# A first stage with its loads in another order and a ring of three, and a joining stage with modulation columns made by one transpose

## The chip, the cores and the metric

The kernel runs on one core of a Trainium2 chip. The metric is the device time of one execution in microseconds (us), lower is better. Its engines are TensorE (PE in the rows, PEld its weight loads), VectorE (DVE), ScalarE (ACT), GpSimd (POOL) and SyncE (SP). SP only issues transfers, ACT and POOL issue some of theirs.

## What the kernel computes

Two layers of a hybrid backbone over 512 latent tokens (rows of `x`) and 256 context tokens (`ctx`), each row 1024 wide, all in float32. Each layer has two sub-layers, and ahead of each of them the rows are normalised and modulated by values computed from a conditioning vector:

```
def rmsnorm(x, g):
    y = xf * lax.rsqrt(jnp.mean(xf * xf, axis=-1, keepdims=True) + EPS)
    return (y * g.astype(jnp.float32)).astype(x.dtype)

def modulate(h, shift, scale):
    return h * (1.0 + scale) + shift
...
def ab_mixer(...):
    pc = jnp.split((hc @ w_in).astype(jnp.float32), AB_SPLITS, axis=-1)
    pl = jnp.split((hl @ w_in).astype(jnp.float32), AB_SPLITS, axis=-1)
...
def mla_project(h, w_in, q_g, kv_g, w_uq, w_ukv, cs):
    p = h @ w_in
...
def hier_moe(...):
    return (jax.nn.silu(xb @ w_gate[e]) * (xb @ w_up[e])) @ w_down[e]
```

The modulation values (`mods`: per layer six vectors of 1024, once for the latent stream and once for the context stream) are the product of silu(c) with `ada_w`, which has 1024 x 6144 entries per layer, plus `ada_b`. Layer 0 is the retention and RG-LRU mixer followed by a mixture of 32 experts with two per token. Layer 1 is latent attention (MLA) followed by a second mixture. The output of a mixture goes back into the stream as `x = x + gate * (w0*y0 + w1*y1)`, where `y0` and `y1` are the rows of the token's two experts.

## The kernel before

Stages follow one another, each in a `Scope` that ends with a barrier of all engines: `ab_project` (the first stage), retention, output projection, routing and experts of layer 0, `combine` of layer 0 (here the joining stage), MLA, routing and experts of layer 1, `combine` of layer 1. A tile is 128 tokens: tiles 0 and 1 are context, 2 to 5 latent. `c.X` holds the six tiles of the stream, `hT` the normalised rows transposed (model dimension on partitions).

**First stage, `ab_project`.** It computes three things. (1) The modulation columns of the first sub-layer: `ada_step(kk, buf)` multiplies silu(c) with one chunk of `ada_w` (1 MB), eight chunks (round 0, `ada_first`) to 2048 columns. The result gets its bias (L713), is transposed (L568) and becomes `scale` and `shift` (L717, L719). (2) The rows: ACT squares each of the six tiles (L629) and takes the root after three tiles and after six (L631), DVE makes the inverse root and scales the tile into `xn` (L703), PE transposes it (L555, `x_transposes`), ACT and DVE copy it out into `hT` (L635, L706). `after` says behind which ada chunk PE has the transposes of which tile. Then L642 (ACT) and L727 (DVE) multiply `hT` by `scale` and add `shift`. (3) The projection in 40 groups, in the fixed order of `groups`: first 16 channel groups (L587; blocks 4 and 5 of `ab_w_in`, context with 256 and latent with 512 columns in turn), then 24 row groups (L583). `BEFORE` says behind which row groups PE has the gate matmuls (L602) of the RG-LRU units, whose scans run on DVE.

The other 40 chunks of `ada_w` (rounds 1 to 5) go through a ring of buffers in `c.X`, whose rows are no longer needed once they are scaled (SP waits for `scaled`). `ADA_AT[n]` is the index of the group behind which PE takes chunk n. SP walks through the groups in the same order: when chunk n is used, it issues chunk n + RING into the freed buffer, and `clear_slots(n)`, 384 KB of zeros written to `ys`.

SP's queue at the start is: eight ada chunks, the small loads of `tables.sync` (two of them `lru_lambda`, turned to columns by the transfer itself, element by element), weight blocks 0 and 1 (2 MB each, L437), nine more small loads of that kind (`cw`, `gb`), `cs`, the wait for `scaled`, ring chunks 0 and 1, the gate weights. ACT's queue has `c`, `c_ctx`, the six tiles of rows (3 MB, `load_rows`), biases and `gcol`.

**Joining stage, `combine` of layer 0.** Per tile: POOL gathers two rows per token from `ys` (L2228, three buffers), ACT weighs the first (L2244), DVE adds the second (L2269), multiplies by the gate (L2271), adds to `c.X` (L2272). `NormModulate` then normalises: ACT L158 and L161, DVE L94 to L99 and L267 (multiplies with the inverse root and with (1 + scale) * g, laid out in rows of 1024 on all partitions, `mb`, prepared by L255), POOL L276 adds the shift, PE transposes (L289), ACT copies out both halves (L298, L305). DVE has for tile t the three operations of the join, then `scale` of tile t-1. The next stage begins when the last copy is done and the barrier is passed.

## Time and profile before

| | us |
|---|---|
| median of 3 executions | 2185.58 |
| lowest and highest | 2184.8, 2187.6 |
| the profiled execution, its own time | 2187.3 |
| its span in the profile | 2185.6 |

In the span PE is busy for 1713.1 us (78%), DVE for 705.5 us, ACT for 435.5 us, POOL for 259.8 us, and the 16 DMA engines move 260 GB/s on average. The mean granted clock of TensorE is 0.899 of full speed. Shares are averages over stages of different kinds. The rows below cut out two stages: the first one up to 381 us, and the joining one from 1118 to 1187 us.

### The profile page before, as it was taken

How to read it: one execution, taken by the hardware profiler on the slowest of the kernel's cores; microseconds unless marked ns; L12 is line 12 of the kernel's file. 1: busy time of each engine (PE TensorE's matmuls, PEld its weight loads, DVE VectorE, ACT ScalarE, POOL GpSimd, SP SyncE). 2: the span in 40 equal slices, each digit the busy share in tenths (PEclk: the TensorE clock that was granted, in tenths of full speed). 3: DMA queues.
4: the chain of work that ended last, by engine and by line, in shares of the span. 5: the costliest groups of instructions: out<-in, count | busy, mean ns of one | idle time of the engine just before them, and what ended most of it. 6: DMA issues, size and time to landing. Idle time of an engine off the chain costs nothing. (4 is left out here: it accounts for less than half of the span.)

```text
span 2185.6 us, 25873 instructions
## 1 busy us (share of the span) xinstructions
PE 1713.1 (78%) x9070; PEld 895.1 (41%) x9071; DVE 705.5 (32%) x1254; ACT 435.5 (20%) x802; POOL 259.8 (12%) x350
## 2 busy tenths in 40 slices
PE   5999999799499789998614899999938789855651
PEld 2443344645244334444303545555434334433330
DVE  2403675633311111112136227776331111111114
ACT  3102323311001110111113114554101101111112
POOL 1002350301100000001013110000111000000001
PEclk8999999899599999999865899999958999987885
DMA  9767653500799999999963002000169999999993
GB/s 320 239 246 250 217 175 120 199 26 39 315 385 361 413 418 412 424 398 403 419 269 123 2 0 87 1 1 8 54 254 389 414 410 406 413 413 410 414 413 137
DMA packets 105452, 568.10 MB, mean 260 GB/s; under 512 B 22728, under 2 KB 40904, under 8 KB 65568
## 3 DMA queue, kind: packets, MB, share of 16 engines
q1 hardware_dynamic: 90544, 521.94, 60.5%
q0 software_dynamic: 7744, 26.22, 3.4%
q10 hardware_dynamic: 7088, 18.92, 2.2%
q8 instruction: 48, 0.79, 0.1%
q14 instruction: 28, 0.23, 0.0%
HBM read 525.55 MB, written 41.50 MB: 259 GB/s over the span
## 5 line engine op out<-in xcount | busy, mean ns | idle before, releaser
L1927 PE MATMUL exp_gps<-moew_wg,all_hT 128*64 128x512 f32 (+1 forms) x480 | 238.6, 621 | 35.4 <-DMA moew_wu<-in_moe_w_up 33.1
L1921 PE MATMUL exp_gps<-moew_wg,all_hT 128*32 128x256 f32 x1088 | 160.5, 460 | 104.3 <-DMA moew_wu<-in_moe_w_up 97.9
L1928 PE MATMUL exp_ups<-moew_wu,all_hT 128*64 128x512 f32 (+1 forms) x480 | 237.3, 618 | 0.0
L583 PE MATMUL abp_ps<-ab_w,all_hT 128*128 128x512 f32 x384 | 169.6, 597 | 0.6 <-PE abp_ps L587 0.3
L1921 PE MATMUL exp_ups<-moew_wu,all_hT 128*32 128x256 f32 x1088 | 160.2, 460 | 0.0
L1921 PEld LDWEIGHTS exp_gps<-moew_wg,all_hT 128*32 128x32 f32 x1088 | 79.1, 131 | 182.5 <-issue 139.0
L1927 PEld LDWEIGHTS exp_gps<-moew_wg,all_hT 128*64 128x64 f32 (+1 forms) x480 | 77.7, 166 | 169.7 <-issue 169.7
L1955 PE MATMUL exp_yps<-moew_wd,all_hT 128*64 128x512 f32 (+1 forms) x240 | 117.3, 606 | 20.4 <-issue 20.4
L2047 DVE TENSOR_TENSOR all_hT<-all_hT,exp_ups 64x512 f32<-64x512 f32 (+1 forms) x30 | 20.7, 690 | 343.6 <-ACT all_hT L1997 343.6
L1957 PE MATMUL exp_yps<-moew_wd,all_hT 128*64 128x512 f32 (+1 forms) x240 | 116.8, 603 | 0.0
L583 PEld LDWEIGHTS abp_ps<-ab_w,all_hT 128*128 128x128 f32 x384 | 71.6, 190 | 98.5 <-issue 98.3
L1421 PE MATMUL att_sc<-mla_KT,mlak_QT 96*128 96x384 f32 x256 | 100.5, 517 | 2.0 <-PEq L75 2.0
L1928 PEld LDWEIGHTS exp_ups<-moew_wu,all_hT 128*64 128x64 f32 (+1 forms) x480 | 78.5, 166 | 50.9 <-issue 50.9
L1884 POOL COPY exp_idx<-all_tok 128x1 int32 (+1 forms) x64 | 11.7, 182 | 734.9 <-DVEq L2034 734.2
L2045 DVE TENSOR_TENSOR all_hT<-all_hT,exp_ups 64x256 f32<-64x256 f32 x34 | 14.4, 425 | 253.7 <-ACT all_hT L1995 253.7
L1905 PE MATMUL exp_xps<-all_ident,all_hT 128*128 128x128 f32 x512 | 74.5, 290 | 24.8 <-DMA all_hT<-h_rows,exp_idx 24.8
L587 PE MATMUL abp_ps<-all_hT,ab_w 128*128 128x256 f32 (+1 forms) x256 | 89.4, 506 | 1.3 <-DVE all_hT L727 1.0
L1905 PEld LDWEIGHTS exp_xps<-all_ident,all_hT 128*128 128x128 f32 x512 | 64.3, 194 | 58.3 <-issue 33.2
L1949 PE MATMUL exp_yps<-moew_wd,all_hT 128*32 128x256 f32 x1088 | 69.0, 395 | 14.8 <-issue 12.1
L1493 DVE TENSOR_REDUCE att_nmax<-att_sc 128x1 f32<-128x768 f32 x64 | 61.3, 957 | 50.2 <-PE att_sc L1421 50.2
L1997 ACT ACTIVATE all_hT<-exp_gps 64x512 f32<-64x512 f32 (+1 forms) x30 | 17.8, 593 | 298.3 <-PE exp_ups L1928 298.3
L2064 DVE COPY exp_y<-exp_yps 64x512 f32<-64x512 f32 (+1 forms) x30 | 20.8, 693 | 163.2 <-PE exp_yps L1957 163.2
(399 smaller groups left out, 2572.0 us busy)
## 6 DMA issues: line engine op xcount, KB each, us to landing
moew_wg<-in_moe_w_gate SPq DMA_DIRECT2D x64, 2048.0 KB, 24.7
moew_wu<-in_moe_w_up SPq DMA_DIRECT2D x64, 2048.0 KB, 30.0
moew_wd<-in_moe_w_down SPq DMA_DIRECT2D x64, 2048.0 KB, 31.3
all_X<-in_ada_w SPq DMA_DIRECT2D x40, 1024.0 KB, 6.2
ab_w<-in_ab_w_in SPq DMA_DIRECT2D x6, 2048.0 KB, 9.1
ys<-abp_zero SPq DMA_DIRECT2D x32, 384.0 KB, 7.1
ys<-exp_y ACTq DMA_DIRECT2D x13, 512.0 KB, 8.7
ab_rows<-in_ada_w SPq DMA_DIRECT2D x6, 1024.0 KB, 12.0
```

What stands on the lines that cost most here:

```text
L583: last = nc.tensor.matmul(ps[i % RB][:], hT[:, kk, what * P:(what + 1) * P], w[n % S][:, kk, :], start=(kk == 0), stop=(kk == KD - 1))
L587: last = nc.tensor.matmul(ps[i % RB][:, 0:m], w[n % S][:, kk, ct * P:(ct + 1) * P], hT[:, kk, o:o + m], start=(kk == 0), stop=(kk == KD - 1))
L1421: last = nc.tensor.matmul(sc[n % 2][:, b, 0:HALF], k.QT[0:QD, h, t * P:(t + 1) * P], k.KT[0:QD, h, b * HALF:(b + 1) * HALF], start=True, s ...
L1493: V.tensor_reduce(nmax[:, n % R:n % R + 1], sc[n % 2][:, :, 0:HALF], mybir.AxisListType.XY, ALU.max, negate=True).then_inc(mx, 1)
L1905: last = nc.tensor.transpose(xps[k // 4][:, k % 4, :], x_by[q][:, k, :], c.ident[:])
L1921: last = nc.tensor.matmul(bank[lo + j * Q:lo + (j + 1) * Q, 0:HC], x[:, k, 0:Q], wt[:, k, j * HC:(j + 1) * HC], start=(k == 0), stop=(k == ...
L1927: nc.tensor.matmul(gps[0:rows, :], x[:, k, 0:rows], w.g[q][:, k, :], start=(k == 0), stop=(k == KD - 1))
L1928: last = nc.tensor.matmul(ups[at:at + rows, :], x[:, k, 0:rows], w.u[q][:, k, :], start=(k == 0), stop=(k == KD - 1))
L1949: last = nc.tensor.matmul(yps[j // 2][j * Q:(j + 1) * Q, 0:HC], hT[:, k, 0:Q], w.d[q][:, k, j * HC:(j + 1) * HC], start=(k == 0), stop=(k ...
L1955: nc.tensor.matmul(yps[0][0:rows, :], hT[:, k, 0:rows], w.d[q][:, k, 0:512], start=(k == 0), stop=(k == HT_N - 1))
L1957: last = nc.tensor.matmul(yps[1][at:at + rows, :], hT[:, k, 0:rows], w.d[q][:, k, 512:1024], start=(k == 0), stop=(k == HT_N - 1))
L2064: nc.vector.tensor_copy(y[q][0:rows, 512:1024], yps[1][at:at + rows, :]).then_inc(y_dve, 1)
```

## The change

The text calls it new attention together with the first stage in another order and a new joining stage. The diff has nothing in the attention itself.

- `ab_project`: the rows are loaded first on SP's queue, ahead of the ada chunks, and no longer on ACT's. Weight block 0 comes directly behind the ada chunks. The ring has three buffers, and `ADA_AT` places the eight chunks of a round behind five groups as 1, 2, 2, 2, 1 and no longer 2, 2, 2, 1, 1. The transposes of the rows stand earlier among the ada steps (`after`).
- The small parameters (`gcol`, `cw`, `gb`, `lru_lambda`) are loaded as contiguous rows into one tile `laid` (56 x 128) by five transfers of ACT's queue, transposed by one PE instruction and copied once by DVE into `pcols`. PE has the wait for these loads at the head of its queue, ahead of all ada steps, and DVE waits for the transpose ahead of its first inverse.
- `combine_into_mla` takes the place of `combine` for layer 0. ACT multiplies the tile by its inverse root, PE transposes it, ACT copies both halves out, and scale and shift are applied to `hT` afterwards by columns, odd columns on ACT and even ones on DVE, context after the context tiles, latent at the end. The columns come from one transpose of `laid` (40 x 128). POOL only gathers, and `mb` and its preparation are gone.

```diff
-        cw = s.sb("cw", [P, CONV + 1, LT])
-        gb = s.sb("gb", [P, 4, LT])
+        NG = KD
+        NW = NG + CONV * LT
+        NC = NW + LT
+        NB = NC + 4 * LT
+        NL = NB + 2 * LT
+        laid = s.sb("laid", [NL, P])
+        pcols = s.sb("pcols", [P, NL])
+        gcol = pcols[:, 0:NG]
+        cw = pcols[:, NG:NC].rearrange("p (t c) -> p t c", c=LT)
+        gb = pcols[:, NC:NB].rearrange("p (d c) -> p d c", c=LT)
+        lam = pcols[:, NB:NL]
...
-        RING = 2
+        RING = 3
...
+        laid_cols = gates_ctx[:].rearrange("p g n -> p (g n)")[:, 0:NL]
...
-        ADA_AT = [2 + 7 * r + r // 4 + at for r in range(ROUNDS - 1) for at in (0, 0, 1, 1, 2, 2, 3, 4)]
+        ADA_AT = [2 + 7 * r + r // 4 + at for r in range(ROUNDS - 1) for at in (0, 1, 1, 2, 2, 3, 3, 4)]
...
+            load_rows(sp, c, a, x_in)
             for kk in range(KD):
                 ada_chunk(0, kk, ada_first[kk], first_ready[kk])
+            block_of(0)
             tables.sync(sp)
-            block_of(0)
             block_of(1)
-            for t in range(CONV):
-                sp.dma_start(cw[:, t, :], a["lru_conv_w"][0, t].rearrange("(c p) -> p c", p=P),
-                             allow_slow_non_contiguous=True).then_inc(p_ready, 16)
-            sp.dma_start(cw[:, CONV, :], a["lru_conv_b"][0].rearrange("(c p) -> p c", p=P),
-                         allow_slow_non_contiguous=True).then_inc(p_ready, 16)
-            for dg in range(4):
-                sp.dma_start(gb[:, dg, :], a["lru_gate_b"][0, dg // 2, dg % 2].rearrange("(c p) -> p c", p=P),
-                             allow_slow_non_contiguous=True).then_inc(p_ready, 16)
+            sp.wait_ge(scaled, NT)
+            for n in range(RING):
+                ring_chunk(n)
             sp.dma_start(cs[:], a["ret_cs"]).then_inc(cs_ready, 16)
-            sp.wait_ge(scaled, NT)
-            ring_chunk(0)
-            ring_chunk(1)
...
-            after = {2: (0,), 3: (1,), 4: (2,), 5: (3, 4), 6: (5,)}
+            after = {0: (0, 1), 1: (2,), 2: (3,), 3: (4,), 4: (5,)}
+            pe.wait_ge(p_ready, 16 * 5)
+            nc.tensor.transpose(laid_cols, laid[:], c.ident[0:NL, 0:NL]).then_inc(laid_tr, 1)
             pe.wait_ge(silu_done, 1)
...
-            load_rows(act, c, a, x_in)
+            act.dma_start(laid[0:NG, :], a["norm_g"][0, 0].rearrange("(k p) -> k p", p=P)).then_inc(p_ready, 16)
+            act.dma_start(laid[NG:NW, :], a["lru_conv_w"][0].rearrange("t (c p) -> (t c) p", p=P)).then_inc(p_ready, 16)
+            act.dma_start(laid[NW:NC, :], a["lru_conv_b"][0].rearrange("(c p) -> c p", p=P)).then_inc(p_ready, 16)
+            act.dma_start(laid[NC:NB, :], a["lru_gate_b"][0].rearrange("d g (c p) -> (d g c) p", p=P)).then_inc(p_ready, 16)
+            act.dma_start(laid[NB:NL, :], a["lru_lambda"][0].rearrange("d (c p) -> (d c) p", p=P)).then_inc(p_ready, 16)
             act.wait_ge(zeroed, 3)
             load_bias(act, 0, bias0, b0_ready)
             load_bias(act, 1, bias, b_ready)
-            act.dma_start(gcol[:], a["norm_g"][0, 0].rearrange("(k p) -> p k", p=P),
-                          allow_slow_non_contiguous=True).then_inc(g_ready, 16)
...
-            act.wait_ge(p_ready, 16 * (CONV + 5))
+            act.wait_ge(cols_set, 1)
...
             V.memset(eps[:], EPS).then_inc(eps_set, 1)
+            dve.wait_ge(laid_tr, 1)
+            V.tensor_copy(pcols[:], laid_cols).then_inc(cols_set, 1)
+            dve.wait_ge(cols_set, 1)
             for n, lo in enumerate((0, NT // 2)):
                 cols = slice(lo, lo + NT // 2)
...
-            dve.wait_ge(g_ready, 16)
             dve.wait_ge(mod_tr, 1)
...
     def sync(sp):
         sp.dma_start(z[:, 0:2 * RH], a["ret_decay_logit"].rearrange("o d h -> o (d h)")
                      .to_broadcast([P, 2 * RH])).then_inc(ready, 16)
-        for d in range(2):
-            sp.dma_start(z[:, 2 * RH + d * LT:2 * RH + (d + 1) * LT],
-                         a["lru_lambda"][0, d].rearrange("(c p) -> p c", p=P),
-                         allow_slow_non_contiguous=True).then_inc(ready, 16)
...
-        dve.wait_ge(ready, 48)
+        dve.wait_ge(ready, 16)
         dve.wait_ge(io, 6)
+        link(V.tensor_copy(z[:, 2 * RH:], lam))
         link(V.tensor_scalar(z[:], z[:], -1.0, None, ALU.mult))
...
-        if layer + 1 < DEPTH:
-            norm = NormModulate(nc, c, a, s, layer + 1, 0, t0, tile_done, pairs=2)
-        else:
-            norm = FinalNorm(nc, c, a, s, t0, tile_done)
+        norm = FinalNorm(nc, c, a, s, t0, tile_done)
...
+def combine_into_mla(nc, c, a, r, prefetch):
+    T = NT
+    layer = 0
+    PARTS = ((1, 0, CTX), (0, CTX, SEQ))
+    with Scope(nc, f"comb{layer}") as s:
+        YB = 3
+        y = [[s.sb(f"y{b}{k}", [P, DM]) for k in range(2)] for b in range(YB)]
+        got = [s.sem(f"got{b}") for b in range(YB)]
+        gate = s.sb("gate", [P, 2, DM])
+        gs, ex = s.sb("gs", [P, T]), s.sb("ex", [P, T])
+        xn = [s.sb(f"xn{i}", [P, DM]) for i in range(2)]
+        laid = s.sb("laid", [5 * KD, P])
+        cols = s.sb("cols", [P, 5, KD])
+        tp = [s.ps(f"tp{i}", [P, 4, P]) for i in range(4)]
+        cps = s.ps("cps", [P, 5, KD])
+        (gate_ready, weighed, x_done, chain, exp_done, w_done, laid_ready, cols_tr, cols_done, rstd_done, scaled, tr, ev_act,
+         aff) = (s.sem(n) for n in (
+             "gate_ready", "weighed", "x_done", "chain", "exp_done", "w_done", "laid_ready", "cols_tr", "cols_done",
+             "rstd_done", "scaled", "tr", "ev_act", "aff"))
+        norm = RowNorm(nc, c, a, s, 0, lambda eng, t: eng.wait_ge(x_done, t + 1), s.sb)
+        block = s.block()
+        @block.sync
+        def _(sp):
+            for st in range(2):
+                sp.dma_start(laid[2 * st * KD:(2 * st + 2) * KD, :],
+                             c.mods[st, 1, 0:2 * DM].rearrange("(k p) -> k p", p=P)).then_inc(laid_ready, 16)
+            sp.dma_start(laid[4 * KD:, :], a["norm_g"][1, 0].rearrange("(k p) -> k p", p=P)).then_inc(laid_ready, 16)
+            load_gates(sp, c, gate, gate_ready, layer, 1, 2)
+            sp.wait_ge(got[0], 32)
+            prefetch(sp)
+        @block.gpsimd
+        def _(pool):
+            for t in range(T):
+                if t >= YB:
+                    pool.wait_ge(x_done, t - YB + 1)
+                for k in range(2):
+                    nc.gpsimd.indirect_dma_start(y[t % YB][k][:], None, c.ys[:, :],
+                                                 bass.IndirectOffsetOnAxis(r.slot[:, k * T + t:k * T + t + 1], 0)
+                                                 ).then_inc(got[t % YB], 16)
+        @block.scalar
+        def _(act):
+            nc.scalar.activation(r.gshift[:, 0:T, :], r.gshift[:, 0:T, :], ACT.Exp).then_inc(exp_done, 1)
+            nc.scalar.activation(ex[:], r.eshift[:, 0:T], ACT.Exp).then_inc(exp_done, 1)
+            act.wait_ge(w_done, 1)
+            def weigh(t):
+                act.wait_ge(got[t % YB], 32 * (t // YB + 1))
+                nc.scalar.mul(y[t % YB][0][:], y[t % YB][0][:], r.w[:, 0, t:t + 1]).then_inc(weighed, 1)
+            def scale(t):
+                act.wait_ge(rstd_done, t + 1)
+                if t >= 2:
+                    act.wait_ge(tr, 2 * (t - 2) + 2)
+                nc.scalar.mul(xn[t % 2][:], c.X[:, t, :], norm.rstd[:, t:t + 1]).then_inc(scaled, 1)
+            def evict(t):
+                for half in range(2):
+                    act.wait_ge(tr, 2 * t + half + 1)
+                    nc.scalar.copy(c.hT[:, 4 * half:4 * half + 4, t * P:(t + 1) * P], tp[2 * (t % 2) + half][:]).then_inc(ev_act, 1)
+            def by_columns(half):
+                st, o, m = PARTS[half]
+                act.wait_ge(cols_done, 2)
+                act.wait_ge(ev_act, 2 * (o + m) // P)
+                for kk in range(1, KD, 2):
+                    nc.scalar.activation(c.hT[:, kk, o:o + m], c.hT[:, kk, o:o + m], ACT.Identity,
+                                         scale=cols[:, 2 * st + 1, kk:kk + 1], bias=cols[:, 2 * st, kk:kk + 1]).then_inc(aff, 1)
+            weigh(0)
+            weigh(1)
+            for t in range(T):
+                norm.square(act, t)
+                if t >= 1:
+                    scale(t - 1)
+                if t >= 2:
+                    evict(t - 2)
+                if t + 2 < T:
+                    weigh(t + 2)
+                if t == T - 1:
+                    by_columns(0)
+            scale(T - 1)
+            evict(T - 2)
+            evict(T - 1)
+            by_columns(1)
+        @block.vector
+        def _(dve):
+            link = Chain(dve, chain)
+            V = nc.vector
+            V.memset(norm.eps[:], EPS).then_inc(norm.eps_set, 1)
+            def by_columns(half):
+                st, o, m = PARTS[half]
+                dve.wait_ge(ev_act, 2 * (o + m) // P)
+                for kk in range(0, KD, 2):
+                    V.tensor_scalar(c.hT[:, kk, o:o + m], c.hT[:, kk, o:o + m], cols[:, 2 * st + 1, kk:kk + 1],
+                                    cols[:, 2 * st, kk:kk + 1], ALU.mult, ALU.add).then_inc(aff, 1)
+            def inverse(t):
+                norm.inverse(dve, link, t)
+                dve.sem_inc(rstd_done, 1)
+            dve.wait_ge(exp_done, 2)
+            link(V.tensor_reduce(gs[:], r.gshift[:, 0:T, :], AX, ALU.add))
+            link(V.scalar_tensor_tensor(out=gs[:], in0=ex[:], scalar=1.0, in1=gs[:], op0=ALU.add, op1=ALU.mult))
+            link(V.reciprocal(r.w[:, 0, 0:T], gs[:]))
+            V.tensor_tensor(r.w[:, 1, 0:T], r.w[:, 0, 0:T], ex[:], ALU.mult).then_inc(w_done, 1)
+            dve.wait_ge(cols_tr, 1)
+            link(V.tensor_copy(cols[:], cps[:]))
+            for st in range(2):
+                V.scalar_tensor_tensor(out=cols[:, 2 * st + 1, :], in0=cols[:, 2 * st + 1, :], scalar=1.0, in1=cols[:, 4, :],
+                                       op0=ALU.add, op1=ALU.mult).then_inc(cols_done, 1)
+            dve.wait_ge(w_done, 1)
+            dve.wait_ge(cols_done, 2)
+            dve.wait_ge(gate_ready, 32)
+            for t in range(T):
+                st = 1 if t < CT else 0
+                y0, y1 = y[t % YB]
+                dve.wait_ge(weighed, t + 1)
+                link(V.scalar_tensor_tensor(out=y0[:], in0=y1[:], scalar=r.w[:, 1, t:t + 1], in1=y0[:],
+                                            op0=ALU.mult, op1=ALU.add))
+                link(V.tensor_tensor(y0[:], y0[:], gate[:, st, :], ALU.mult))
+                V.tensor_tensor(c.X[:, t, :], c.X[:, t, :], y0[:], ALU.add).then_inc(x_done, 1)
+                if t >= 1:
+                    inverse(t - 1)
+            inverse(T - 1)
+            by_columns(0)
+            by_columns(1)
+        @block.tensor
+        def _(pe):
+            pe.wait_ge(laid_ready, 48)
+            nc.tensor.transpose(cps[:].rearrange("p a k -> p (a k)"), laid[:], c.ident[0:5 * KD, 0:5 * KD]).then_inc(cols_tr, 1)
+            for t in range(T):
+                pe.wait_ge(scaled, t + 1)
+                for half in range(2):
+                    if t >= 2:
+                        pe.wait_ge(ev_act, 2 * (t - 2) + half + 1)
+                    for j in range(4):
+                        kk = 4 * half + j
+                        last = nc.tensor.transpose(tp[2 * (t % 2) + half][:, j, :], xn[t % 2][:, kk * P:(kk + 1) * P], c.ident[:])
+                    last.then_inc(tr, 1)
...
-            combine(nc, c, a, 0, 0, r, lambda sp: load_w_in(sp, a, k))
+            combine_into_mla(nc, c, a, r, lambda sp: load_w_in(sp, a, k))
             mla_layer(nc, c, a, k)
         moe_rows(nc, c, a, 1, CT, r)
         combine(nc, c, a, 1, CT, r)
```

## Rows read from the trace of the kernel before

**Rows 1.** Windows: length, busy us of each engine, PEclk, DMA share, GB/s.
```profile
2.00:45.00 43.00, 19.88 (x112) 9.19 (x112) 10.44 (x26) 13.69 (x23) 6.83 (x12) 0.80 0.99 367
45.00:381.00 336.00, 319.55 (x1028) 140.55 (x1028) 151.54 (x156) 84.73 (x136) 66.26 (x46) 0.98 0.62 208
...
1118.00:1187.00 69.00, 11.81 (x48) 9.41 (x48) 48.05 (x67) 24.47 (x40) 31.67 (x18) 0.50 0.49 184
```

**Rows 2.** Waits of PE, 0 to 420 us: us in total, times, longest.
```profile
PE abp_aps L544 <- DMA all_X<-in_ada_w: 12.3, 9, 2.4
```

**Rows 3.** DMA issues, 0 to 60 us: count, KB each, us from issue to landing.
```profile
abp_x<-in_ada_w SPq DMA_DIRECT2D x1, 1024.0 KB, 26.9
...
abp_craw<-in_c_ctx ACTq DMA_DIRECT2D x1, 4.0 KB, 7.3
...
abp_gcol<-in_norm_g ACTq DMA_DIRECT2D x1, 4.0 KB, 24.9
```

**Rows 4.** Line L437, weight blocks 0 and 1: landing after issue.
```profile
DMA to landing us min/median/max: 16.6/18.7/20.8
```

**Rows 5.** Timeline 0 to 90 us: start, duration, what.
```profile
6.52 0.49 SPq L442 DMA_DIRECT2D abp_x<-in_ada_w  x1
...
12.01 4.52 PE L544 MATMUL abp_aps<-ab_rows,abp_sT 128*32 128x512 f32 x24 [12.01 <-ACT abp_sT L623]
...
19.51 13.57 SPq L437 DMA_DIRECT2D ab_w<-in_ab_w_in  x2
...
28.66 1.94 PE L544 MATMUL abp_aps<-ab_rows,abp_sT 128*32 128x512 f32 x8
...
33.91 1.06 ACT L629 ACTIVATE abp_ri<-all_X 128x1024 f32<-128x1024 f32 x1 [3.27 <-DMA all_X<-in_x]
...
42.60 1.09 PE L555 MATMUL abp_ps<-all_ident,abp_ri 128*128 128x128 f32 x8
...
43.63 1.06 PE L544 MATMUL abp_aps<-abp_x,abp_sT 128*32 128x512 f32 x8
...
47.26 14.01 PE L587 MATMUL abp_ps<-all_hT,ab_w 128*128 128x256 f32 x48 [1.02 <-DVE all_hT L727]
```

**Rows 6.** Timeline of PE alone, 60 to 420 us.
```profile
83.39 9.04 PE L587 MATMUL abp_ps<-all_hT,ab_w 128*128 128x512 f32 x16
...
98.00 7.13 PE L587 MATMUL abp_ps<-all_hT,ab_w 128*128 128x512 f32 x16
```

**Rows 7.** Window of 4 us at the first of them.
```profile
84.00:88.00 4.00, 4.00 (x7) 1.57 (x6) 3.73 (x6) 0.00 (x0) 0.13 (x1) 0.59 1.02 369
```

**Rows 8.** Ring chunks (tile all_X), 40 to 420 us: landing.
```profile
DMA to landing us min/median/max: 5.2/7.0/16.6
```

**Rows 9.** Joining stage by line and form: busy us, mean ns, idle before.
```profile
L276 POOL TENSOR_TENSOR comb_nh<-comb_nh,comb_nmb 128x1024 f32<-128x1024 f32 x6 | 17.9, 2986 | 23.1 <-DVE comb_nh L267 23.1
L2271 DVE TENSOR_TENSOR comb_y<-comb_y,comb_gate 128x1024 f32<-128x1024 f32 x6 | 15.4, 2572 | 0.2
...
L267 DVE SCALAR_TENSOR_TENSOR comb_nh<-all_X,comb_nrstd,comb_nmb 128x1024 f32<-128x1024 f32 x6 | 7.7, 1284 | 0.2
...
L2244 ACT ACTIVATE comb_y<-comb_y,all_w 128x1024 f32<-128x1024 f32 x6 | 6.9, 1147 | 10.3 <-DMA comb_y<-ys,all_slot 10.3
```

**Rows 10.** The joining stage of layer 1 (no work on POOL), DVE, by line.
```profile
L2271 DVE TENSOR_TENSOR comb_y<-comb_y,comb_gate 128x1024 f32<-128x1024 f32 x4 | 4.9, 1224 | 0.1
```

**Rows 11.** Timeline of the joining stage: tiles 1 and 5 joined, last copy.
```profile
1136.14 1.23 DVE L2272 TENSOR_TENSOR all_X<-all_X,comb_y 128x1024 f32<-128x1024 f32 x1
...
1173.89 1.22 DVE L2272 TENSOR_TENSOR all_X<-all_X,comb_y 128x1024 f32<-128x1024 f32 x1
...
1186.27 0.59 ACT L305 COPY all_hT<-comb_ntp 128x512 f32<-128x512 f32 x1 [0.27 <-PE comb_ntp L289]
```

**Rows 12.** Line L2228, the gathers of layer 0: landing after issue.
```profile
DMA to landing us min/median/max: 5.0/7.7/9.6
```

**Rows 13.** First stage by form, 45 to 52 us: modulation by columns.
```profile
L642 ACT ACTIVATE all_hT<-all_hT,abp_shift,abp_scale 128x512 f32<-128x512 f32 x4 | 2.9, 798 | 0.0
```

10 lines of the change are left out of this document (4 added, 6 removed).

## The prediction, made before the changed kernel was run

> **What bounds the kernel now.** The chain that ended last is of no use here: it reaches back only some 40 us, into the last stage. I read the kernel by stages instead, with a table of windows [rows 1]. The first stage has two halves. Up to 45 us the DMA engines are busy for 99% of the time and PE for less than half: that half is bound by bytes and by the order in which they come. From 45 to 381 us PE is busy for 319.6 of 336 us while DMA is at 62%: PE sets the end. The list of PE's waits says what its idle time is: 12.3 us in nine pieces, each for a ring chunk of `ada_w` [rows 2]; no other wait inside the 40 groups is above 1 us. In the joining stage DVE is busy for 48 of 69 us, PE for 12, DMA for half: DVE's chain sets the pace there [rows 1]. The stages behind are not touched, and each begins after a barrier, so time saved in these two should come through whole.
>
> **First stage, up to the first group.** The order is read off the timeline [rows 5]. The sixth tile of rows is squared only at 33.9 us, as the rows share the DMA engines with 8 MB of ada chunks from SP's queue. Its transposes run at 42.6 us, and PE, which takes its work in order, has the last ada step behind them at 43.6 us. The first group starts at 47.26 us, 2.6 us after that step has ended (bias, transpose, columns, first multiplication of `hT`). The last chunk itself had landed at 6.5 + 26.9 = 33.4 us [rows 3, 5], so ten us go to waiting behind the rows.
>
> After the change the rows come first: 3.1 MB at the some 420 GB/s that DMA shows here are 7.5 us, so the last tile is there at about 12 us. ACT's silu is done at 12.0 us, when PE begins [rows 5], and comes a little earlier with fewer issues ahead; three squares of 1.25 us, a table load, the roots and DVE's inverse and scaling, 7 us in all, and PE can transpose tile 0 at about 18.7 us. The bytes ahead of the last chunk are the same as before, so it lands again at 33.4 us. PE has until then six tiles of transposes and seven steps. At the full clock that is 6 x 1.09 + 7 x 1.06 = 14 us and fits in the 14.7 us from 18.7 to 33.4; with some 4 us more for the first pieces at the low clock the last step ends at about 35.6 us. The group could start at 38.2 us. It needs weight block 0, which before landed at 19.5 + 20.8 = 40.3 us [rows 4, 5]; it has the same bytes ahead of it less the `lru_lambda` loads, element by element, at which DMA fell to half its rate for about 3 us. I take 38.8 us for it and 39.0 us for the first group: **8.2 us less**. The bounds are 9 us (the group as soon as the columns are ready) and nothing (first rival).
>
> The parameters cost five issues on ACT of some 0.45 us, fewer than the six of the rows that leave, and one transpose and one DVE copy (below 0.7 us each, in the shade of the chunks). All of PE stands behind their landing. They are issued by 6.1 us; a small load on ACT's queue took 7.3 us when nothing stood ahead of it and 24.9 us behind the rows [rows 3]. Nothing large stands ahead now, so I take the first: 13.4 us, before chunk 0 is there (about 15 us) and before DVE needs its first root (16.6 us). Cost zero; if that cover is gone, each us is one on the path.
>
> **First stage, the groups.** Two prices come with the waits. The direct one is 12.3 us [rows 2]. The other is the clock: a latent channel group takes 7.13 us at full clock, but 9.04 us behind a pair of waits [rows 6], and in the window there the granted clock is 0.59, a mixture of 1.2 and 2.4 GHz [rows 7]. There are two such places, 1.9 us each, and in each one ada step took 1.94 us and not 1.06 (both lengths in [rows 5]), 0.9 us more. Together 5.6 us.
>
> With three buffers and the order 1, 2, 2, 2, 1, chunk n + 3 is issued when chunk n is used. In round 0, counted from the first group, the chunks are used at 14.5 (one), 22.7 (two), 28.5 (two), 37.8 (two) and 43.5 us. A ring chunk takes 5.2 us at least and 7.0 in the middle from issue to landing [rows 8]. The tightest is chunk 4, issued at 23.8 and wanted at 29.6: 5.8 us, so 0 to 1.2 us remain. Round 1 has one such place too (5.9 us); in rounds 2 to 4 every group takes 7.13 us and the tightest distance is over 9 us. A pause of about 1 us alone did not lower the clock before. I leave 1.1 us of waits in all: 12.3 + 5.6 - 1.1 = **16.8 us less**. DMA can carry it: in round 0 five chunks and seven clearings, 8 MB in 29 us, are 275 GB/s. DVE is not near its own bound: it is busy for 152 of the 336 us [rows 1], and its work keeps its place between PE's groups.
>
> **Joining stage.** Before, a tile costs DVE 1.28 (L2269) + 2.57 (L2271) + 1.22 (L2272) + 1.28 (L267) + 1.17 (six small ones) and little gaps; in the steady part L2271 is 3.25 and the period 8.1 us. L2271 is that long because POOL adds the shift meanwhile: without work on POOL the same form takes 1.22 us [rows 9, 10]. The change takes away L267, L276 and so the long form: 3.73 + 1.17 = 4.9 us a tile, and ACT has 1.54 (square and root) + 1.15 (scale) + 1.18 (two copies) + 1.15 (weigh) = 5.0 us. I take 4.95. From the join of tile 1 (ended 1137.4) to that of tile 5 (ended 1175.1) it was 37.7 us [rows 11] and becomes 4 x 4.95 = 19.8: 17.9 less. The start to tile 1 is the same. The tail grows: after tile 5's join ACT squares it (1.5), scales tile 4 and copies tile 3 out (2.3), does four context columns (4 x 0.6 at most), scales tile 5 and copies tile 4 out (2.3), waits for PE's transposes at the low clock and copies twice (1.8), and does four latent columns at 0.80 [rows 13], 3.2 us: 13.4 us against 1186.9 - 1175.1 = 11.8 before [rows 11]. Sum: 17.9 - 1.6 = **16.3 us less**. The column transpose and its copies lie under the first gathers (about 8 us of idle DVE). Bounds: 17.9 if the tail costs nothing, 12 by the third rival.
>
> **Sum.** 8.2 + 16.8 + 16.3 = 41.3 us. The profiled execution took 2187.3, so 2146.0; it lies 1.7 us above the median of the three runs, from which the same subtraction gives 2144.3. I say 2145.
>
> **Rivals.**
> - *The start stays at the low clock.* At 1.2 GHz an ada step takes 1.94 us [rows 5] and a tile's transposes about twice 1.09. The granted clock has a mean of 0.80 up to 45 us [rows 1]. If PE stayed low from 18.7 us on, the last step would end at 18.7 + 6 x 2 + 7 x 1.94 = 44.3 us and the group begin at 47: nothing of the 8.2 us is left, 2153. For it speaks that the new order hands PE its chunks at intervals of 2.6 us. Against it: by my times PE runs without a pause from 18.7 to about 32 us, as it has arrears, and before, it had gone from the long step at 28.7 us to the short one at 43.6 us with more pauses than that [rows 5]. The Trainium skill (TensorE: Matmul & The Clock Gate, "HAM oscillation") says that short bursts between waits for DMA keep falling back to the low clock; by that rule this rival would hold and 2153 be the time, by the rows it holds only if the arrears run out early.
> - *The ring is still short.* Clearings and gate weights share the engines with chunks; DMA's share at the waits is 1.02 [rows 7]. If half of the waits and one fall of the clock remain, 6 + 2.7 us come back: 2152.
> - *The joining stage waits for gathers.* The buffer of tile t is free after the join of tile t-3, which leaves two periods and an inverse, 11.1 us, for two issues (1.25 us apart), a landing of 7.7 us in the middle and 9.6 at most [rows 12], and the weighing: 10.1 to 12.0. At the upper end three tiles are 0.9 late, and as ACT, in order, then holds its copies back as well, up to 4.5 us: 2149.
> - *Slower: the head of PE's queue.* If the five small loads land late, everything is late. The nearest row for late is 24.9 us [rows 3], that is a landing near 31 us, and the first group at about 53: 14 us worse than planned, still 27 us faster overall. It turns into a loss only from a landing of 15 + 41 = 56 us, for which no row speaks; 2190 then.
> - *Nothing comes of it.* The later stages would have to take the time back, as the experts wait for weights whose transfers begin with their stage. They begin after the barrier, so I see no way.
>
> **How the numbers follow.** My forecast (2140 to 2150) 0.57; low clock 0.16; ring 0.09; gathers 0.12; loss 0.03; nothing 0.03. The range goes from 2139, all three savings at their upper bounds (9 + 17.8 + 17.9 = 44.7, from the median 2141, and 2 for the executions' own spread), to 2158, the first two rivals partly together. A run of this kernel can be told from no change at about 0.2%, 4.4 us; all cases but the last two lie beyond. Faster 0.94, same 0.03, slower 0.03.
>
> **What the profile would show.** The first L587 at 38 to 40 us (47 by the first rival, with L544 at 1.94 throughout). PE's waits for `all_X<-in_ada_w` at 2 us or less, and no group of L587 at 9 us. The first stage's end at about 355 us. L2271 at 1.22 us, periods of 5 us, and 53 us instead of 69 for the joining stage. I am wrong if PE's first instruction comes after 16 us, or if PE waits for something new among the groups: DVE's units or the weight blocks.

## The result, and the profile after

The changed kernel takes 2152.23 us (median of 4 runs, 2148.22 to 2155.07), the kernel before, run beside it, 2185.19 us (4 runs, 2182.76 to 2187.6). The ratio is 0.9848, with a 95% interval of 0.9827 to 0.9868. The forecast was 2145 in a range of 2139 to 2158. The sign and the range were right; 33 of the 41 us came. The narrower case to which the forecast gave 0.57 (2140 to 2150) did not come.

The profiled execution took 2153.72 us, its span is 2152.0. Cut at the same events as before (first group; last group's end; first issue of the joining stage; first issue of the stage behind it), the two spans differ so. The forecast for the two untouched stretches was no change:

| stretch | before | after | saved | forecast |
|---|---|---|---|---|
| up to the first group | 47.26 | 40.13 | 7.1 | 8.2 |
| the 40 groups | 332.58 | 321.96 | 10.6 | 16.8 |
| groups' end to joining stage | 738.11 | 739.70 | -1.6 | 0 |
| joining stage | 69.73 | 53.30 | 16.4 | 16.3 |
| behind it | 997.92 | 996.91 | 1.0 | 0 |

Most of what is missing (6.2 of 7.7 us) is missing among the groups. The windows of the kernel after, to be read against [rows 1], in the same columns:

```profile
2.00:40.00 38.00, 18.17 (x117) 8.17 (x117) 12.41 (x34) 14.66 (x26) 6.84 (x12) 0.92 0.97 378
40.00:362.00 322.00, 315.81 (x1024) 140.80 (x1024) 149.28 (x150) 82.99 (x133) 66.15 (x46) 0.99 0.65 221
1102.00:1155.00 53.00, 12.13 (x49) 9.59 (x49) 32.00 (x69) 34.68 (x54) 12.96 (x12) 0.50 0.50 191
```

PE is busy for 316 of the 322 us of the groups; DVE's busy time in the joining stage fell from 48 to 32 us, while ACT's rose from 24.5 to 34.7, so DVE and ACT now share the pace. PE's waits up to 420 us, against [rows 2] (us in total, times, longest):

```profile
PE abp_gpsc L563 <- DMA abp_laid<-in_lru_lambda: 10.9, 1, 10.9
...
PE abp_aps L546 <- DMA ab_rows<-in_ada_w: 5.3, 1, 5.3
PE abp_aps L546 <- DMA all_X<-in_ada_w: 4.7, 2, 3.3
...
PE abp_aps L546 <- DMA abp_x<-in_ada_w: 2.0, 1, 2.0
...
PE abp_ps L591 <- DVE all_hT L735: 1.7, 1, 1.7
...
PE abp_aps L546 <- DMA ab_yT<-in_ada_w: 1.1, 1, 1.1
```

L546 is the ada step (L544 before). Nine waits for ring chunks (`all_X`) have become two, 12.3 us have become 4.7. New are pauses for the last two first chunks (`ab_yT`, `abp_x`). The timeline of the start, against [rows 5]:

```profile
9.79 0.43 SPq L451 DMA_DIRECT2D abp_x<-in_ada_w  x1
...
10.89 0.34 PE L563 MATMUL abp_gpsc<-all_ident,abp_laid 52*128 52x52 f32 x1 [10.89 <-DMA abp_laid<-in_lru_lambda]
...
18.41 2.70 PE L557 MATMUL abp_ps<-all_ident,abp_ri 128*128 128x128 f32 x16
...
31.39 1.06 PE L546 MATMUL abp_aps<-ab_yT,abp_sT 128*32 128x512 f32 x8 [1.11 <-DMA ab_yT<-in_ada_w]
...
34.49 1.94 PE L546 MATMUL abp_aps<-abp_x,abp_sT 128*32 128x512 f32 x8 [2.04 <-DMA abp_x<-in_ada_w]
...
37.31 1.11 PE L572 MATMUL abp_gps<-all_ident,abp_gt 128*128 128x128 f32 x4 [0.89 <-DVE abp_gt L722]
...
40.13 15.84 PE L591 MATMUL abp_ps<-all_hT,ab_w 128*128 128x256 f32 x48 [1.70 <-DVE all_hT L735]
```

The small loads are there at 10.9 us, before anything needs them (the line of L563 also shows that `laid` has 52 rows and not 56), and PE begins the transposes at 18.41 us (18.7 by the forecast). The last chunk comes at 34.5 us (9.79 + 24.7 from issue to landing; the forecast had 33.4) and its step takes 1.94 us, the length at 1.2 GHz; the transposes behind it take 1.11 us where e6 below has 0.66. The first 48 instructions of the groups take 15.84 us where [rows 5] has 14.01. Windows of the same stretch:

```profile
31.00:34.00 3.00, 1.06 (x8) 0.16 (x8) 0.00 (x0) 0.00 (x0) 0.00 (x0) 0.94 0.98 388
34.00:37.00 3.00, 1.94 (x8) 0.20 (x8) 0.43 (x1) 0.00 (x0) 0.00 (x0) 0.50 1.05 388
...
40.00:43.00 3.00, 2.87 (x7) 2.34 (x8) 2.80 (x10) 3.00 (x6) 0.00 (x0) 0.50 1.06 388
43.00:46.00 3.00, 3.00 (x13) 2.37 (x12) 0.00 (x0) 1.05 (x3) 0.00 (x0) 0.86 1.06 426
```

The granted clock (third number from the right) is 0.94 while PE does one step in three us, then 0.50, which is 1.2 GHz, until some us after the groups have begun. The Trainium skill (TensorE: Matmul & The Clock Gate, "HAM oscillation") says that bursts separated by waits for DMA fall back to the low clock; the trace agrees here, where a burst of 1.06 us stood between waits of 1.11 and 2.04 us.

The two places with ring waits in PE's timeline, against [rows 6]:

```profile
71.95 1.06 PE L546 MATMUL abp_aps<-all_X,abp_sT 128*32 128x512 f32 x8 [1.42 <-DMA all_X<-in_ada_w]
72.95 7.13 PE L591 MATMUL abp_ps<-all_hT,ab_w 128*128 128x512 f32 x16
...
127.85 1.06 PE L546 MATMUL abp_aps<-all_X,abp_sT 128*32 128x512 f32 x8 [3.27 <-DMA all_X<-in_ada_w]
128.84 8.83 PE L591 MATMUL abp_ps<-all_hT,ab_w 128*128 128x512 f32 x16
```

The first is the tight place of round 0 that the forecast named, and it leaves the clock alone. The second, in round 1, is 3.27 us long and is followed by a group of 8.83 and not 7.13 us. Its chunk was issued at 119.13 us and landed at 127.8: 8.7 us, where the forecast had reckoned with 5.2 to 7.0.

### The profile page after: what moved, and what is told of

It is laid out like the page before. It is cut to its first block and busy times, and to the rows that moved or that the text cites. A ratio compares the mean times of both kernels' runs of the same rounds, so it can differ in the third digit from the quotient of the medians.

```text
span 2152.0 us, 25890 instructions
## 1 busy us (share of the span) xinstructions
PE 1710.2 (79%) x9072; PEld 896.6 (42%) x9073; DVE 689.1 (32%) x1259; ACT 445.5 (21%) x816; POOL 241.4 (11%) x344
```

## The experiments

"T0" is the start of the first group. The stretches are read from each kernel's profile at the events of the table above. Together the two stretches that no kernel here touches (groups' end to joining stage, and behind the joining stage) took 1730.7 to 1738.4 us in the twelve profiled executions, 1736.0 before and 1736.6 after. That is the spread of code that is the same everywhere, and a stretch tells a difference better than a median does, but for the first stage not to the last microsecond. In e1 and e7, which have the first stage of the kernel before, the first group begins at 45.87 and 47.18 us (47.26 before), the groups take 330.4 and 330.9 us (332.6) and end at 376.3 and 378.1 us (379.8). Against these two the new first stage saves 14.2 and 16.0 us, against the profile of the table 17.7. The joining stage is steadier: seven profiles of the new one lie between 53.2 and 53.7 us.

**e1 and e2: one half of the change each.** e1 has only the new joining stage, e2 only the new first stage.

```diff
 e1, on the kernel before:
-            combine(nc, c, a, 0, 0, r, lambda sp: load_w_in(sp, a, k))
+            combine_into_mla(nc, c, a, r, lambda sp: load_w_in(sp, a, k))
 e2, on the kernel after:
-            combine_into_mla(nc, c, a, r, lambda sp: load_w_in(sp, a, k))
+            combine(nc, c, a, 0, 0, r, lambda sp: load_w_in(sp, a, k))
```

Expected of e1:

> The kernel before with the new joining stage alone. My theory: the two parts are independent, since each ends at a barrier; the joining stage lasts 53.3 us from its first issue to the first issue of the next stage, as in the changed kernel, where it was 69.7 before, and the whole comes out 16.4 us under the kernel before (2169). The rival, that part of the gain belongs to the stages in between or behind, would show as a total that is off by more than 3 us while the stage itself is 53 us long.

Expected of e2:

> The changed kernel with the old joining stage: the first stage's part alone. My theory: first group at 40.1 us, last group of the first stage ended near 362 us, 17.7 us earlier than before, and the whole about 17 us under the kernel before (2168). Together with the run of the joining stage alone it should give the full change, 33 to 34 us. The rival, that the first stage gives more than its 17.7 us and the stages between take some back (they were 1.6 us longer in the changed kernel), expects the stages between to be longer here too by 1.6 us; if that was the spread of one execution, it has gone or has the other sign.

e1 took 2168.89 us (ratio 0.9923, 0.9897 to 0.995), e2 2169.54 (0.9928, 0.9901 to 0.9955), the kernel before beside them 2185.32. They save 16.4 and 15.8 us, together 32.2; the whole change saves 33.0. The halves add up within their intervals, so nothing is given back between them. That e2 saves 15.8 us and not the 17.7 of the table fits the spread of the old first stage. The joining stage is 53.7 us long in e1 (53.3 after), the groups in e2 321.7 (322.0 after).

**e3: the ring of two with the old places of the chunks, all else as after.**

```diff
-        RING = 3
+        RING = 2
-        ... for at in (0, 1, 1, 2, 2, 3, 3, 4)]
+        ... for at in (0, 0, 1, 1, 2, 2, 3, 4)]
```

> The changed kernel with a ring of two and the old placement of the chunks (2, 2, 2, 1, 1), rows still first. My theory: the start does not depend on the ring, so the first group begins at 40 us; the waits for ring chunks return to about 12 us with a fall of the clock in two places, and the stage from first to last group is 332 us as before (322 with the ring of three): 10 us slower than the changed kernel. The rival, that the order of the loads helped the groups as well (the small column loads are gone from the queue), expects less than that, 326 us or under.

The groups take 333.3 us, as before the change (332.6), with nine ring waits again:

```profile
PE abp_aps L546 <- DMA all_X<-in_ada_w: 10.4, 9, 2.4
```

T0 stays at 40.4 us, and the time is 2161.0 (0.9891, 0.9856 to 0.9926). Of the 333.3 us 2.5 are the low clock at the start of the groups (their first 48 instructions take 16.50 us where [rows 5] has 14.01), so the rest is 1.8 us shorter than before. What the groups gained comes from the third buffer and the new places together, which were not tried apart, and the order of the start gives its 7 us without them.

**e4: the clearings behind the ring.** `clear_slots` no longer goes out beside the first sixteen ring chunks but from chunk 16 on, two at a time.

```diff
-                        clear_slots(n)
+                        if n >= 16:
+                            for b in range(2 * (n - 16), min(2 * (n - 16) + 2, BLOCKS)):
+                                clear_slots(b)
...
-            for b in range(len(ADA_AT), BLOCKS):
-                clear_slots(b)
```

> The changed kernel with the clearing transfers moved away from rounds 0 and 1: none beside chunks 0 to 15, then two beside each of chunks 16 to 37. Same work. My theory: chunks 4 and 14 come late (1.4 and 3.3 us of waiting) because the DMA engines serve the clearings, which are writes in pieces of 1 KB and cost more of the engines' time than their bytes say; without them the chunk lands within 5.5 us of its issue, both waits fall under 0.5 us, the clock stays up (7.1 us and not 8.8 for the group behind), and the groups take 6 us less, 316 us. The rival, that the distance of 5.5 us from issue to use is too short for a chunk on any terms (the fastest landing was 5.3 us, with 16 engines shared by the next chunk), expects both waits to stay at 1 us or more, and a new wait in rounds 2 to 4, where two clearings now stand beside each chunk.

The time is 2145.41 us (0.9819, 0.9783 to 0.9855). PE waits for no ring chunk at all, and the groups take 315.5 us, 6.5 less than after: the 4.7 us of waits and the 1.7 us of the slow group. So the clearings beside the chunks are what makes them late. Windows of 2 us in which the late chunk of the kernel after was under way, one of after and two of e4 (last three numbers: clock, DMA share, GB/s):

```profile
120.00:122.00 2.00, 2.00 (x10) 1.77 (x11) 0.00 (x0) 0.00 (x0) 0.00 (x0) 1.00 0.90 205
```

```profile
120.00:122.00 2.00, 2.00 (x10) 1.54 (x9) 0.00 (x0) 0.00 (x0) 0.00 (x0) 1.00 1.02 426
...
124.00:126.00 2.00, 2.00 (x7) 0.99 (x6) 0.00 (x0) 0.00 (x0) 0.00 (x0) 1.00 0.97 315
```

In the first pair the engines are almost as busy with half the bytes. This is no measure of what a clearing costs: e4 has a window of 315 GB/s at a share of 0.97 with no clearing under way, and over the whole way of the late chunk, 118 to 128 us, the kernel after moves 327 GB/s at a share of 0.95, e4 351 at 0.93. SP's queue in the kernel after shows what was under way:

```profile
119.13 0.33 SPq L451 DMA_DIRECT2D all_X<-in_ada_w  x1
119.50 0.58 SPq L459 DMA_DIRECT2D ys<-abp_zero  x1
...
120.78 2.02 SPq L459 DMA_DIRECT2D ys<-abp_zero  x1
```

A clearing is 384 KB in pieces of 1 KB, and adds that much to each chunk of 1 MB. In the trace's records of single packets a piece of 1 KB took 46 ns and one of 8 KB, of which the chunks are made, 309 ns in the middle, so 1 KB pieces took 1.2 times as long for the same bytes. e4 takes the bytes away together with the pieces; which of the two makes the chunk late was not tried. The landing times of the ring chunks from 42 to 150 us, in the kernel after and in e4:

```profile
DMA to landing us min/median/max: 5.3/9.0/11.2
```

```profile
DMA to landing us min/median/max: 4.5/5.1/9.2
```

Behind 150 us, beside the clearings, chunks of e4 take up to 12.4 us, and no wait comes of it.

**e5: PE kept busy before the first group.** Extra transposes of the identity into a spare bank fill PE's pauses: 8, 16 and 6 behind the last three steps, 10 behind the modulation transposes. It is extra work, whose results nobody reads.

```diff
+                keep_busy({5: 8, 6: 16, 7: 6}.get(kk, 0))
...
             last.then_inc(mod_tr, 1)
+            keep_busy(10)
```

> The changed kernel with 40 extra transposes of the identity on PE into a bank that nobody reads: 8 before chunk 6 is waited for, 16 before chunk 7, 6 before the bias is added and 10 behind the transposes of the modulation. Extra work, same result. My theory: PE's pauses of 1.1 and 2.0 us before the last two chunks let the clock fall, which costs 0.9 us in the last step, 0.5 in the transposes and 1.8 us in the first groups (15.8 us for the first 48 matmul records, 14.0 at the full clock). With the pauses filled the last step is 1.06 us and the first groups take 14.0 us; the first group begins at 39 to 40 us, since weight block 0 lands at about 40; the groups take 320 us and the whole is 2 to 3 us faster than the changed kernel. The rival, that the first groups are slow for another reason (DMA is at its full rate there), expects 15.8 us again, and a later start by what the extra transposes cost.

```profile
40.65 14.01 PE L598 MATMUL abp_ps<-all_hT,ab_w 128*128 128x256 f32 x48 [1.79 <-DVE all_hT L742]
```

The last step took 1.06 us, the first 48 instructions 14.01 and not 15.84: the clock is held. The columns of `hT` begin at 38.16 us and not at 38.82, yet T0 did not come earlier (40.65): the slow steps ahead of it are not what sets it. The releaser that the line names had long been done; the last part of weight block 0 landed at 40.37 us. Of the ring waits one is left (3.8 us), and the groups take 320.5 us, 1.4 less than after (after, e2 and e8, alike in this stage, have 321.7 to 322.9). The time is 2146.12 us (0.9825, 0.9808 to 0.9843), 6 under the kernel after, but the touched stretches account for 0.7 of it; the untouched ones took 1730.7 us in this profile, the least of all. So e5 shows the 1.8 us of the first 48 instructions and no more; the rest of its lower median is in no stretch that it touches.

**e6 and e10: the rows behind the chunks again**, on ACT's queue and with the old places of the transposes; e6 on the kernel after, e10 on e4.

```diff
-            load_rows(sp, c, a, x_in)
+            load_rows(act, c, a, x_in)
-            after = {0: (0, 1), 1: (2,), 2: (3,), 3: (4,), 4: (5,)}
+            after = {2: (0,), 3: (1,), 4: (2,), 5: (3, 4), 6: (5,)}
```

> The changed kernel with the rows back on the queue of ACT, behind the five parameter loads, and with the old place of their transposes among the steps. My theory: the whole gain of the start comes from the rows being first, so the first group begins at 45.5 to 46.5 us (the column loads are still gone, which is worth about 1 us) and the rest stays as it is, 322 us of groups. 5 to 6 us slower than the changed kernel. The rival, that the missing column loads made the gain (DMA fell to half its rate for some 3 us at them), expects 42 us or less.

> The changed kernel with the rows loaded behind the chunks again, on ACT's queue, and the clearings late. Question: does loading the rows first pay once the ring has no waits? My theory, that the rows' order costs the 1.8 us of clock at the first group and the rest was the ring's luck: first group at 45.7 us, groups 313.7 us (315.5 less 1.8), so the first stage ends 3.6 us later than with late clearings alone, 2149. Rival, that the order of the rows is indifferent, as it was with the early clearings: the end of the groups within 1 us of 355.8, 2145.4.

e6 took 2151.94 us (0.9845, 0.9826 to 0.9864), no worse than the kernel after by the median, where 5 to 6 us more were expected; its first stage ends 2.3 us later (364.4 against 362.1). T0 is 5.6 us later, as expected, which refutes the rival of the column loads, but the groups are 3.3 us shorter, which was not expected: 1.8 of it is the clock, 1.5 the ring waits, of which 3.2 us stand against 4.7. e10 took 2149.49 us (0.9846, 0.9828 to 0.9865) and settles it. Without ring waits the groups take 313.8 us at the warm start, and the stage ends at 359.4 us, 3.7 later than in e4 (355.8). The first 48 instructions in e10 (14.01 us in e6 too):

```profile
45.65 14.01 PE L590 MATMUL abp_ps<-all_hT,ab_w 128*128 128x256 f32 x48 [0.95 <-DVE all_hT L735]
```

So loading the rows first, with their transposes earlier among the steps, brings 5.3 us at T0 (45.65 - 40.31), and gives 1.7 back in clock (315.5 - 313.8), since PE then meets the last chunks with nothing else to do. With the rows late PE has transposes up to the end and goes warm into the groups.

**e7: the joining stage of before without POOL's add.** The shift is left out but for its first column (the kernel leaves that part of the modulation out), all else as before.

```diff
-        h = self.h[:, t % self.HB, :]
-        self.nc.gpsimd.tensor_add(h, h, self.mb[:, st, 0, :]).then_inc(self.h_done, 1)
+        n = 1 if self.layer == 1 and self.sub == 0 else DM
+        h = self.h[:, t % self.HB, 0:n]
+        self.nc.gpsimd.tensor_add(h, h, self.mb[:, st, 0, 0:n]).then_inc(self.h_done, 1)
```

> The kernel before, in whose joining stage of layer 0 POOL adds the shift to one column of 1024 only; the rest of the shift is left out. My theory: half of what the new joining stage gives is the long form of DVE's multiplication by the gate, 3.25 us beside POOL's addition and 1.22 without. The period goes from 8.1 to 6.1 us, the tail loses the 2.3 to 3.3 us of the addition before the last transposes, and the stage takes 58 to 60 us where it took 69.7. The rival, that DVE's multiplication is long for another reason (the gathers write meanwhile), expects 3.2 us for it again, and only the tail shorter.

The stage takes 56.7 us, 13.0 less than before, by leaving out this one add (one run, 2170.67 us): 8.1 of it between join 1 and join 5, 4.1 behind join 5, 0.8 ahead of join 1. The new stage is 3.4 us shorter still, but in another way: 8.8 us less than e7 between join 1 and join 5 (20.9 against 29.7), and 4.6 us more behind join 5 (13.0 against 8.4) and 0.8 more ahead of join 1. By line and form in the joining stage of e7, and of the kernel after (busy us, mean ns, idle before):

```profile
L2272 DVE TENSOR_TENSOR comb_y<-comb_y,comb_gate 128x1024 f32<-128x1024 f32 x6 | 7.3, 1224 | 0.2
...
L277 POOL TENSOR_TENSOR comb_nh<-comb_nh,comb_nmb 128x1 f32<-128x1 f32 x5 | 4.8, 969 | 21.3 <-DVE comb_nh L267 21.3
```

```profile
L2411 DVE TENSOR_TENSOR comb_y<-comb_y,comb_gate 128x1024 f32<-128x1024 f32 x6 | 7.3, 1224 | 0.2
```

DVE's gate multiplication (L2271 in [rows 9], mean 2572 ns) takes 1224 ns in both. In e7 its period is 6.07 us (8.1 before, 4.98 after), and L267 is still in it. The Trainium skill (GPSIMD Engine Reference, "8. Key points") says that GpSimd shares its SBUF interfaces with VectorE and contends with its instructions that have two SBUF inputs; the trace agrees: 1224 ns alone, 2572 in the mean beside POOL's add. The mean hides two values, and the timeline shows what the long one is made of (before, then e7):

```profile
1145.20 3.31 POOL L276 TENSOR_TENSOR comb_nh<-comb_nh,comb_nmb 128x1024 f32<-128x1024 f32 x1 [8.29 <-DVE comb_nh L267]
1146.35 3.25 DVE L2271 TENSOR_TENSOR comb_y<-comb_y,comb_gate 128x1024 f32<-128x1024 f32 x1
```

```profile
1154.82 1.28 DVE L2270 SCALAR_TENSOR_TENSOR comb_y<-comb_y,all_w 128x1024 f32<-128x1024 f32 x1
1154.99 1.16 POOL L277 TENSOR_TENSOR comb_nh<-comb_nh,comb_nmb 128x1 f32<-128x1 f32 x1 [1.61 <-DVE comb_nh L267]
...
1169.47 0.19 POOL L277 TENSOR_TENSOR comb_nh<-comb_nh,comb_nmb 128x1 f32<-128x1 f32 x1 [2.16 <-DVE comb_nh L267]
```

Before, POOL's add ends at 1148.51 us and DVE's multiplication 1.09 us later, as if it had begun only then; the other three pairs do the same. It goes the other way too: in e7 POOL's add of one column, begun beside DVE's L2270, takes 1.16 us and ends with it, and 0.19 us where no such instruction runs. Behind join 5 before, a DVE operation on one column (L96), begun beside an add, takes 2.13 us and ends with it, where it takes 0.16 us elsewhere. By these times each engine stood still until the other's instruction was through.

**e8: the attention's input weights later.** `load_w_in` waits for the second join and not for the first gather, to free DMA for the gathers.

```diff
-            sp.wait_ge(got[0], 32)
+            sp.wait_ge(x_done, 2)
             prefetch(sp)
```

> The changed kernel in whose joining stage the 2.6 MB of the next stage's weights are issued after the join of tile 1 and not after the first gather. My theory: the gathers of tile 3 came late (ACT waited 3.3 us for them, DVE 1.1 us) because they share the engines with that load; with it later, ACT's wait is under 1 us, and the stage is 1 us shorter, 52.3 us, no more, since the period of 5 us is DVE's own. The rival, that the gather takes 7 to 8 us on any terms, expects the wait to stay at 3 us, and the load to disturb the gathers of tiles 4 and 5 instead.

The stage takes 52.9 us, 0.4 less than after, hardly more than the spread of the stage (one run, 2156.22 us, of which the untouched stretches have 1738.4, the most of all). ACT's wait for tile 3's gather fell from 3.3 to 2.2 us, where less than 1 was expected, and 0.8 came up at tile 4, as the rival said. So the loads are a small part of the gathers' lateness. What holds the rest, the buffer or the gathers' own landing, was not taken apart.

**e9: e4, e5 and e8 together.**

> The changed kernel with the clearings behind the last ring chunk, transposes to keep PE busy ahead of the first group, and w_in's loads late in the joining stage. My theory, in which clearings and clock are separate causes: the first group at 40.5 us, its first 48 instructions 14.0 us, no wait for a ring chunk, groups 313.7 us (315.5 less 1.8), the joining stage 52.9; the time 1.8 to 2.2 us under the kernel with late clearings alone (median 2145.4), that is 2143.4. Rival, the clock's warm start is only worth anything because it moves the place of a wait: groups 315.5 and 2145.4.

The time is 2139.93 us (2137.05 to 2141.78, ratio 0.9794, 0.9775 to 0.9812), the fastest kernel here. T0 is 40.31, the groups take 313.77 us, the joining stage 53.06, all as expected; the median is 3.5 us under the expected 2143.4. The two touched stages together are 8.3 us shorter than after and 1.8 shorter than in e4; the further 4 to 5 us under the kernel after lie in the untouched stretches of the two profiles (1731.5 us against 1736.6) and are their spread. At T0 the timeline names what binds now:

```profile
40.31 14.01 PE L598 MATMUL abp_ps<-all_hT,ab_w 128*128 128x256 f32 x48 [1.92 <-DMA ab_w<-in_ab_w_in]
```

PE waits there for weight block 0, as it also did in e2 (at 40.25 us) and e3 (at 40.38). The columns begin at 37.69 us in e9, 1.1 us before those of the kernel after, and T0 is the same. In all seven kernels with the rows first PE starts 0.24 to 0.28 us after the last part of block 0 has landed.

## Why the prediction was right, and where it was off

- **Small loads at the head of PE's queue: right.** They were there at 10.9 us (13.4 forecast) and cost nothing. The slower rival had no ground.
- **First group, 8.2 us: 7.1.** The failed step is "I take 38.8 us" for weight block 0. The last part of it landed at 39.9 us in the kernel after and at 40.0 to 40.4 in the six others with the rows first (40.3 before). The forecast took off 1.5 us for the `lru_lambda` loads that are gone, and in e6 and e10, which lack these loads too, block 0 did land at 38.8 us. What differs there is that the rows go by ACT's queue and that the ring chunks are issued at 40.7 us; in the kernel after they are issued from 29.25 us on, while block 0 is still under way. Block 1 is issued at 29.2 us in e6 and e10 and at 28.8 after, so it is not what makes the difference. At 39.9 us the kernel after had moved some 14.3 MB (summed from windows), when 13.6 MB are all that rows, first chunks and block 0 hold, so engines went to transfers issued behind block 0. That a transfer lands when the bytes ahead of it are through was the wrong model. It also missed the last chunk by the same 1.1 us (34.5 for 33.4). That the ring chunks are the cause is argued from this comparison; no run delayed them alone. The Trainium skill (DMA: Bandwidth & Descriptors, "Rules for kernel authors") says that transfers issued from different engines run on the same 16 DMA engines and interleave; the trace agrees in so far as the rate from 10 to 30 us is the same with the rows on ACT's queue (413 to 425 GB/s) as with all on SP's (410 to 422).
- **Low clock at the start (0.16): not as told.** PE's first step took 1.94 us, and from 21 to 32 us its steps took 1.06, as the forecast held against it. But the arrears ran out before chunks 6 and 7, and the clock fell on the last step. T0 paid nothing for it (e5), the groups 1.8 us (15.84 against 14.01), a cost that the forecast had in no term.
- **Groups, 16.8 us: 10.6.** The failed step is "I leave 1.1 us of waits in all". 4.7 us were left, with one fall of the clock (1.7). The forecast took 5.2 to 7.0 us for a landing, from a ring of two, and the late chunk took 8.7. Behind it stands the sentence that DMA can carry it, "8 MB in 29 us, are 275 GB/s": that is a mean over the round. In the chunk's own 8.7 us SP issued two more chunks and three clearings, and the engines were busy for 0.95. e4 takes the clearings away and gives the 6.5 us back. Without them and with the clock held the groups take 313.8 us (e9), 18.8 less than before: the direct and the clock price (12.3 + 5.6 = 17.9) were sized well, with 0.9 us that no step explains. The rival "the ring is still short" (0.09) told what happened, with 8.7 us lost where it was 6.4. That its 2152 is the measured median is luck: the difference is made up by block 0 and the untouched stretches.
- **Joining stage, 16.3 us: 16.4**, the sum of two terms that were both off by about 1 us, in opposite ways. The mechanism was right (e7); that the sum fits to 0.1 us is luck. Its parts, read in the timeline of the kernel after against [rows 11]:

```profile
1119.99 1.22 DVE L2412 TENSOR_TENSOR all_X<-all_X,comb_y 128x1024 f32<-128x1024 f32 x1
...
1127.14 1.15 ACT L2337 ACTIVATE comb_y<-comb_y,all_w 128x1024 f32<-128x1024 f32 x1 [3.33 <-DMA comb_y<-ys,all_slot]
...
1128.32 1.28 DVE L2409 SCALAR_TENSOR_TENSOR comb_y<-comb_y,all_w 128x1024 f32<-128x1024 f32 x1 [1.08 <-ACT comb_y L2337]
...
1140.86 1.22 DVE L2412 TENSOR_TENSOR all_X<-all_X,comb_y 128x1024 f32<-128x1024 f32 x1
...
1151.34 2.93 ACT L2355 ACTIVATE all_hT<-all_hT,comb_cols 128x512 f32<-128x512 f32 x4
```

  From join 1 to join 5 it is 20.9 us (37.7 before, 19.8 forecast): three periods of 4.98 us, where 4.95 was said, and one that waits 1.08 us on DVE for the gather of tile 3. That is the rival of the gathers, at a quarter of its price: one tile late, not three. The tail from join 5 to the next stage's first issue is 13.0 us against 12.6 before, 0.4 more where 1.6 was said; up to the last column operation it is 12.2 us and not 13.4.
- **Sum.** Of the 7.7 us that are missing (41.3 - 33.6), 1.1 are block 0, 6.2 the clearings and the clock, -0.1 the joining stage, and 0.6 the untouched stretches, which lies within their spread. The first two are read against one profile of the kernel before, whose first stage is the longest of the three on record (e1 and e7 have the others).

## What to carry to other kernels

Whether a ring of buffers is long enough is a matter of the longest landing, not of the mean rate: sum what shares the engines in the time that DMA is busy with it, and move writes for which nothing waits to where no load is waited for. An element-wise add on GpSimd beside two-input work on VectorE costs VectorE's time too: here it held VectorE up by 2.03 us a tile, and scale and shift by columns, in one operation where partitions are channels, did without it. When transfers are reordered to let an engine work through its arrears early, ask what it does in the pauses that this opens before the last one: here they cost 1.8 us of clock, which idle transposes gave back.

## What the runs showed of the hardware

- Ring chunks of 1 MB landed 9.0 us after their issue in the median with zeros written to HBM beside them in pieces of 1 KB, and 5.1 us without (42 to 150 us, after and e4).
- A burst of one step (1.06 us) between pauses of 1.11 and 2.04 us had the clock at 1.2 GHz by 34 us. With other pauses before the last two steps it was not the same: after 0.20 and 2.22 us the last step still took 1.06 us (e2), after 0.40 and 2.37 us it took 1.56 (e3), after 0.78 and 2.10 us 1.94 (e8). In all of them the clock was low at the first group; the first 48 instructions took 16.81, 16.50 and 16.26 us, and 15.84 in the kernel after.
- A POOL add on a single column took 0.19 us, and 1.16 us when begun beside DVE's two-input L2270 (e7); one on 1024 columns took 2.34 us and 3.31 in the same two cases (before). DVE's multiplication took 1.22 us, and 3.25 when begun beside the long add.
